# Moving two small transpose steps, and the copies and scan that go with them, from the middle of a projection group to a group boundary

## The reference

```python
u = rmsnorm_2(h, norm_a_g[i])
proj = u @ w_in_a[i]
q, k, v, f_logit, gate = jnp.split(proj, [...], axis=-1)   # 1024, 1024, 1024, 16, 1024 columns
q = rmsnorm_2(q...); k = rmsnorm_2(k...)                   # per head of 64
log_f = jax.nn.log_sigmoid((f_logit + b_forget[i]).astype(jnp.float32))
...
c = jnp.cumsum(log_f, axis=1)                              # decay sums over 512 tokens, 16 heads
logits = logits + ci[..., :, None] - c_k[..., None, :]     # in fox_attention
```

## Time and profile before

| | |
|---|---|
| median of 3 runs | 1868.83 us (1868.81 to 1870.37) |
| the profiled execution | 1868.83 us, its span 1866.9 us |
| mean granted TensorE clock | 0.951 of full speed |
| PE busy | 1731.6 us, 93% of the span |
| DVE, ACT, POOL busy | 915.0, 711.3, 376.2 us |

### The profile page before, as it was taken

The page is one execution under the profiler, slowest core; times in us unless marked ns, Lnnn a source line. Parts: engine busy times, 40 slices in busy tenths (PEclk is TensorE's granted clock), DMA queues, the critical chain, the costliest instruction groups (busy, mean ns, idle before and its releaser), DMA issues.

```text
span 1866.9 us, 24733 instructions
## 1 busy us (share of the span) xinstructions
PE 1731.6 (93%) x9327; PEld 1348.7 (72%) x9327; DVE 915.0 (49%) x1634; ACT 711.3 (38%) x1587; POOL 376.2 (20%) x498
## 2 busy tenths in 40 slices
PE   6999788998978999999799999999999999798988
PEld 5888557877674555788688888877887767686766
DVE  3783373224544666334443234334655664366661
ACT  3322474122135666422442223223324553334550
POOL 5440143001213566011000000000102340013320
PEclk9999796999987999999899999998999999898979
DMA  6223121333101221423132233223221003120111
GB/s 177 83 93 125 56 68 62 113 105 98 46 12 43 68 59 45 137 91 113 45 108 95 90 96 107 91 90 113 91 92 46 24 24 137 67 91 24 47 46 46
DMA packets 117779, 147.65 MB, mean 79 GB/s; under 512 B 30684, under 2 KB 63732, under 8 KB 117424
## 3 DMA queue, kind: packets, MB, share of 16 engines
q1 hardware_dynamic: 116608, 145.40, 24.3%
q0 software_dynamic: 992, 0.86, 0.4%
q10 hardware_dynamic: 80, 0.02, 0.0%
HBM read 125.24 MB, written 4.24 MB: 69 GB/s over the span
## 4 chain that ended last, share of the span: by engine, by line
PE 81%; DVE 8%; ACT 8%; issue 3%; POOL 1%; DMA 0%; ACTq 0%; DVEq 0%; POOLq 0%
PE ps L1777 58%; PE ps L2211 3%; PE ps L2018 3%; PE ps L2042 2%; PE ps L2168 2%; ACT pb L766 2%; PE ps L2186 2%; PE ps L2131 1%; PE ps L2061 1%; PE ps L2075 1%; DVE qkt L1272 1%; DVE nm L1242 1%; ACT qkt L785 1%; PE ps L2023 1%; ACT pbf L824 1%
## 5 line engine op out<-in xcount | busy, mean ns | idle before, releaser
L1777 PE MATMUL ps<-spl,ht 128*128 128x512 f32 x2496 | 577.8, 394 | 12.4 <-DVE xk L1502 8.5
L1777 PEld LDWEIGHTS ps<-spl,ht 128*128 128x128 f32 x2496 | 474.0, 190 | 113.2 <-DVE xk L1502 9.0
L1051 DVE TENSOR_TENSOR spl<-raw,spl 128x1024 fp32r<-128x1024 f32 x180 | 234.7, 1346 | 514.6 <-ACT spl L644 514.6
L644 ACT ACTIVATE spl<-raw 128x1024 fp32r<-128x1024 f32 x180 | 180.4, 1051 | 594.9 <-PE ps L1777 594.7
L1777 PE MATMUL ps<-ht,spl 128*128 128x512 f32 x1152 | 263.9, 391 | 2.0 <-DVE spl L1051 2.0
L1777 PEld LDWEIGHTS ps<-ht,spl 128*128 128x128 f32 x1152 | 217.6, 189 | 48.2 <-issue 2.9
L1777 PE MATMUL ps<-spl,uu 128*128 128x512 f32 x768 | 174.4, 389 | 0.0
L1777 PEld LDWEIGHTS ps<-spl,uu 128*128 128x128 f32 x768 | 144.2, 188 | 29.9
L1674 POOL TENSOR_TENSOR sq<-qkv 128x2048 f32<-128x2048 f32 (+1 forms) x15 | 51.5, 3436 | 360.9 <-ACT qkv L678 346.3
L766 ACT ACTIVATE pb<-ps,nm 128x512 f32<-128x512 f32 (+1 forms) x192 | 99.6, 528 | 45.6 <-DVE nm L1242 45.6
L1710 POOL TENSOR_TENSOR pb<-pb,rg 128x512 f32<-128x512 f32 (+3 forms) x160 | 112.7, 721 | 7.5
(11 more groups left out here) (293 smaller groups left out, 2082.9 us busy)
## 6 DMA issues: line engine op xcount, KB each, us to landing
raw<-w_in SPq DMA_DIRECT2D x30, 1024.0 KB, 5.2
raw<-w_mlp_up SPq DMA_DIRECT2D x16, 1024.0 KB, 5.2
raw<-w_mlp_down SPq DMA_DIRECT2D x16, 1024.0 KB, 5.0
raw<-w_in_a SPq DMA_DIRECT2D x16, 1024.0 KB, 5.3
stq<-qkv SPq DMA_DIRECT2D x32, 256.0 KB, 2.7
raw<-w_in_b SPq DMA_DIRECT2D x8, 1024.0 KB, 5.4
raw<-w_proj_diff SPq DMA_DIRECT2D x4, 1024.0 KB, 5.1
stq<-qkv SPq DMA_DIRECT2D x32, 128.0 KB, 2.5
```

The source lines that it names most:

```text
L644: act.activation(SPL[:, n % 2, HI, 2 * k:2 * k + 2], RAW[:, n % 2, 2 * k:2 * k + 2], ACT.Copy).then_inc(hi_done, 4)
L1051: dve.tensor_tensor(SPL[:, n % 2, LO, 2 * k:2 * k + 2], RAW[:, n % 2, 2 * k:2 * k + 2], SPL[:, n % 2, HI, 2 * k:2 * k + 2].bitcast(F32), A ...
L1777: last = pe.matmul(PS[:, b0 + b], left[:, x], right[:, y], start=(kt == 0 and i == 0), stop=(kt == UK * g["units"] - 1 and i == 2))
```

## The change

The hook `between` is removed from every `run`. What it called is called elsewhere:

- PE: `narrow_across` is called at the start of group 3 instead of after the first unit of group 2. `forget_across` is called at the start of group 5 instead of after the first unit of group 4, and PE's wait for the scan follows directly behind its four transposes.
- ACT: `narrow_out` is called at the start of `forget`, at group 3, instead of after the first split in group 2.
- DVE: `decay_sums` is called at the start of group 5, instead of after the first split (and `norm_two`) in group 4.

```diff
@@ scalar
             def forget():
+                narrow_out(NARROW_2)
                 act.wait_ge(f_link, 2)
                 act.activation(FL[:, 3], FL[:, 2], ACT.Exp, scale=-1.0).then_inc(small_act, 1)
-            run(RUNS["fox_in"], primed=True, follow=True, at={0: lambda: narrow_hi(1, 16), 3: forget},
-                between={2: lambda: narrow_out(NARROW_2)})
+            run(RUNS["fox_in"], primed=True, follow=True, at={0: lambda: narrow_hi(1, 16), 3: forget})
@@ vector
-            run(RUNS["fox_in"], primed=True, follow=True, at={0: lambda: narrow_lo(1, 16), 3: forget},
-                between={4: decay_sums})
+            run(RUNS["fox_in"], primed=True, follow=True, at={0: lambda: narrow_lo(1, 16), 3: forget, 5: decay_sums})
@@ tensor
                     last = pe.transpose(PS[0:16, FORGET_BANK, P * t:P * t + P], FL[:, 7, t], IDF[:])
                 last.then_inc(f_tr, 1)
-
-            run(RUNS["fox_in"], at={5: lambda: pe.wait_ge(f_link, N_FORGET)},
-                between={2: lambda: narrow_across(NARROW_2, 1), 4: forget_across})
+                pe.wait_ge(f_link, N_FORGET)
+
+            run(RUNS["fox_in"], at={3: lambda: narrow_across(NARROW_2, 1), 5: forget_across})
@@ every run, of the three engines
-                        if u == 0 and k in between:
-                            between[k]()
```

More of the change, by code:

```diff
@@ L699, in root, with run @@
                     act.activation(RT[:, 0:NT * heads], SS[:, 0:NT * heads], ACT.Sqrt).then_inc(n_rt, 1)
-            def run(groups, hold=(), primed=False, follow=False, first=None, at={}, between={}, norm=0):
+            def run(groups, hold=(), primed=False, follow=False, first=None, at={}, norm=0):
                 units = [(g, u) for g in groups for u in range(g["units"])]
@@ L1167, in evict, with run @@
                     dve.tensor_tensor(x, PS[:, b0:b0 + 4], x, ALU.add).then_inc(freed["dve"], 1)
-            def run(groups, primed=False, follow=False, first=None, at={}, between={}, norm=0):
+            def run(groups, primed=False, follow=False, first=None, at={}, norm=0):
                 units = [(g, u) for g in groups for u in range(g["units"])]
@@ L1840, in _, with run @@
                      "skv": (x_lo, 3 * KT), "sob0": (y_lo, 3 * KT)}
-            def run(groups, norm=0, at={}, between={}):
+            def run(groups, norm=0, at={}):
                 for n, g in enumerate(groups):
@@ L1853, in run @@
                             unit(g, u, g["unit"] + u)
-                        if u == 0 and n in between:
-                            between[n]()
                 if norm:
```

## The result

The changed kernel takes 1882.0 us (median of 4 runs, 1880.8 to 1883.2) against 1869.6 us (4 runs, 1868.8 to 1873.1): ratio 1.0062, 95% interval 1.0045 to 1.0081, so 8 to 15 us slower. It was forecast slower, 1877.1 us with a range up to 1880.5: the direction held, the size was too small and the time lies above the range. The profiled execution took 1879.7 us, less than any of the four timed ones, with a span of 1877.8 us, 10.9 us more than the span before.

What follows compares the result with a forecast made beforehand. PE was taken as the bound, busy 111.00 of 111.00 us in the stage. 1868.83 + 6.85 for waits + 1.40 for one clock fall = 1877.1 us, range 1874.4 to 1880.5.

Steps and rivals of the forecast that it cites:

- The two waits: PE idles 2.05 us at group 3's start and 4.3 us at group 5's; net cost 2.14 + 4.71 = 6.85 us.
- the first place: Start of group 3: PE waits for ACT's copy, queued behind a 2.01 us split; cost +2.14 us.
- The 11.30 us from a restart to the next split: At both boundaries: PE's restart to ACT's next split takes 11.30 us at full clock; 10.88 if the refill is free.
- The clock at the short wait: Group 3's start: nothing added for a clock fall behind PE's wait of 2.05 us.
- the rival with both falls: PE's clock falls at the waits before groups 3 and 5: 1877.1 + 1.40 = 1878.5 us; chance 0.20.
- The clock at the long wait: Group 5's start: clock falls once, late in PE's 4.3 us wait, adding 1.40 us; the other trace case gave 2.16.
- a table load: ACT at group 3: Exp's 1.28 us load expected behind the copy; ahead of it, +3.42 us instead of +2.14.
- DVE's `forget` and the Exp behind it: After group 2: both come no later behind the split's start than before, so no cost.
- The store and SP's next load: After the scan: parts stored 7.75 us later relative to the split's start, but hidden, since SP's next load waits for a split.
- The five instructions behind the scan: DVE, making the three parts: end 7.45 us behind ACT's split start, 0.2 us to spare, no cost.
- E: At a unit's end: the moment ACT's split starts; it returns after 10.88 us with nothing between.
- The rest of the trace moved as a whole: Outside the new idle times and clock loss: a sign of being right, the remaining trace shifted together.

Runs made afterwards that it cites:

- PE kept busy: Changed kernel plus matmuls of no use on PE, 8 ahead of group 3 and 18 ahead of group 5: 1878.6 us, ratio 1.0039.
- scan ahead: Changed kernel with DVE's scan and its five followers moved ahead of the second split of group 4: 1876.9 us, ratio 1.0024.
- both ahead: Changed kernel with ACT's copy ahead of group 2's second split and DVE's scan ahead of group 4's second split: 1873.7 us, ratio 1.0008.
- copy-ahead kernel: Changed kernel with ACT's copy for the banks of group 1 moved ahead of the second split of group 2: 1878.4 us, ratio 1.0038.
- the first place alone: Kernel before with only the narrow transposes moved to group 3's start and ACT's copy behind both splits of group 2: 1877.3 us, ratio 1.0029.

## Why the prediction was right or wrong

**The two waits.** Right, in place, releaser and size. The prediction has 2.14 + 4.71 = 6.85 us without the clock. With PE kept busy the same places cost 2.01 + 4.64 = 6.65 us, and the first place without a fall of the clock (scan ahead) costs 2.04. PE's restarts came 2.17 us (1322.21 to 1324.38) and 4.62 us (1369.93 to 1374.55) behind the split's start, against 2.28 and 4.73. The 11.30 us from a restart to the next split also held: 11.30 us with both ahead (1372.15 to 1383.45). That the second wait came out at exactly 4.3 us has some luck in it: the restart was 0.11 us early, and the transposes ended 0.09 us earlier than was worked out, since they begin 0.28 us ahead of the split (1354.52 against 1354.80 before), not 0.19.

**The clock at the short wait: the step that failed.** "For the wait of 2.05 us I add nothing: none of the rows has a wait of this size behind dense work." The lack of a row was taken for a cost of nothing, though the rival with both falls stood beside it. The clock fell at 1.93 us of idle time in three of four profiles, and it cost 1.6 us. The rival with falls at both waits (0.20) is what happened in the profiled execution, in both profiles of the changed kernel.

**The clock at the long wait: mis-sized.** The term was 1.40 us, "the case in which the fall came late in the wait". The fall came in the middle of it: the clock was 0.50 from 1372.4, 2.1 us ahead of the restart, and then for 4.5 us of work. That is the pattern of the second of the two waits of 4.25 us, with its price of 2.16 us. "The clock is 1.00 while it waits" was read wrongly for that one; in the kernel before, its second half is already at 0.50:

```profile
491.10:493.20 2.10, 0.00 (x0) 0.00 (x0) 2.10 (x10) 0.00 (x0) 0.00 (x0) 0.50 0.00 0
```

Measured: 6.72 - 4.64 = 2.1 us. The copy-ahead kernel, with the same wait of 4.30 us, has a shorter low stretch (0.50 for 3.4 us instead of 6.8) and pays 6.21 us, 1.6 for the clock. So both rows were possible. The argument for the lower one (a full-size unit directly ahead) decided nothing, as such a unit stands ahead in both kernels.

With 1.6 and 2.1 us the sum is 6.65 + 3.7 = 10.3 us, which is the 10.34 us of the stage. The Trainium skill ("TensorE: Matmul & The Clock Gate", Part 1) advises against idle gaps of PE above a stated length, and 1.93 us is well below it. The trace does not agree that a gap below it is safe, so here the measurement decides.

**The base and the range.** The sum was set on 1868.83 us, nearly the lowest time of the kernel before: 18 more runs have a median of 1870.7 us, and go up to 1877.5. The range's upper end of 1880.5 is this base with 11.7 us, which does hold the 10.3 us, and the profiled execution (1879.7 us) lies inside; it had no room for the scatter of the runs, and 1.28 of the 11.7 us is for a table load that did not come ahead of the copy. Both ends should have had the scatter, not the lower alone. The base of 1870.7 us with 10.3 us makes 1881.0 us, and the medians were 1882.0 and 1882.8; the last 1.0 to 1.8 us stay open. (The chances also have a slip: slower sums to 0.91 by the rivals, not 0.92.)

**What was costed at nothing.** DVE's `forget` and the Exp behind it: right, the Exp stays behind DVE's two steps. The store and SP's next load: right, no engine shows a wait for them. The five instructions behind the scan: right in effect, not as told. They were to end at E + 7.45, 0.2 us ahead of the end of POOL's squaring. The first cast took 4.19 us instead of 0.42 in every profile with the scan behind the split, beside POOL's squaring and memset, so that the five ended at E + 11.1 (1381.0). `norm_one` was late by some 3.4 us, and it was hidden, as the split at 1387.98 still waited 4.26 us for PE.

**The rest of the trace moved as a whole:** right for the two profiles of the changed kernel, not for the others. Behind the stage the shift of the kernel with PE kept busy grows from 7.0 to 8.9 us in one place, where the FOX attention ends and its output projection begins; it grows by 0.7 us more later, and shrinks by 1.4 us near the end. The windows (columns as in rows 2) are that stretch of the kernel before, of the changed kernel and of the filled kernel, each moved by its own shift:

```profile
1536.00:1556.00 20.00, 15.08 (x102) 11.94 (x101) 12.72 (x27) 10.53 (x28) 3.03 (x5) 0.91 0.40 148
```

```profile
1547.00:1567.00 20.00, 15.07 (x101) 11.99 (x101) 12.68 (x27) 10.53 (x28) 2.98 (x5) 0.91 0.40 148
```

```profile
1543.00:1563.00 20.00, 15.07 (x88) 11.46 (x88) 12.75 (x27) 10.52 (x28) 2.98 (x5) 0.74 0.35 130
```

The code is the same, and PE is busy for 15.1 us in each, but the clock is 0.74 instead of 0.91 and 88 matmuls start instead of 101. The kernel with the first place alone has 0.66 in its stretch. Its end is 6.5 us late though its stage costs 3.6. In the six edited kernels later stages add 1.1 to 2.9 us in this way. Whether the edit's shift does it is not shown, as single runs of one kernel scatter more than that (1868 to 1878 us for the kernel before, 1873 to 1880 for the first place alone). That scatter does go with the clock, by the mean granted clock that every run has: in the 43 runs of the kernel before, the four below 1869 us have 0.951, and the three above 1876 us have 0.944. In which stages it was lost isn't seen, as only one run of each kernel has a profile. Why the clock falls at some waits of 1.93 us and not at others also stays open: the kernels have the same code up to the wait, and the moments of earlier changes of the clock differ (it had last risen 50.4 us ahead of the wait in the one that kept it, and 49.1 us ahead in each of the three that lost it).

## What to carry to other kernels

Where an engine runs its program in order, as ACT did here (the copy's bank was ready at 1322.44, and the copy began at 1324.12 behind the split), work that the bottleneck engine needs at a boundary must be queued ahead of the work that the same boundary releases; a copy of 0.2 us behind a split of 2 us stalls PE by the split. Price a new wait of PE twice, for itself and for the clock behind it, and where no row shows a wait of that length, bound the clock's share from both sides instead of setting it to zero: here 0 or 1.6 us behind a wait of 1.9 us, and 1.6 to 2.2 us behind 4.3 us. Where such a wait can't be removed, matmuls of no use in it can keep the clock (6.65 against 10.34 us in the stage, one profile; 3.2 us of the whole by the ratios).

## What the runs showed of the hardware

A wait of only 1.93 us between dense stretches was followed by 3.4 us at half clock (1.2 GHz) in three of four profiles, while waits of 1.30 us and 0.31 us, in two profiles each, were followed by none.

A DVE cast of 16x512 float32 to bfloat16 took 4.19 us beside POOL's 3.60 us squaring and its memset (it ended at 1378.72, 0.27 us behind the memset's end), and 0.42 us elsewhere. With the scan ahead the casts came first and kept their 0.41 us, and POOL's squaring took 6.04 us instead of 3.60:

```profile
1370.54 0.41 DVE L1455 CAST c<-cum 16x512 bf16<-16x512 f32 x1
...
1372.97 6.04 POOL L1672 TENSOR_TENSOR sq<-qkv 128x2048 f32<-128x2048 f32 x1 [18.16 <-ACT qkv L678]
1373.20 2.34 DVE L1049 TENSOR_TENSOR spl<-raw,spl 128x1024 fp32r<-128x1024 f32 x2
```

The Trainium skill ("SBUF — State Buffer", "SBUF: two separate sides") says that certain DVE instructions and GpSimd share a pair of ports that one of them holds for its whole instruction, while the other is blocked. Both rows fit it in size: the cast ends just behind POOL's work, and POOL's squaring ends 3.47 us behind the end of the two subtractions (1375.54), close to its own 3.60 us, as if it had been held until then. The page's order, by which the first to start holds the ports, is not what the starts show: the squaring began at 1372.97, ahead of the subtractions at 1373.20 (and inside the last cast), and in the changed kernel the memset began 2.97 us behind the cast and still took the 0.95 us that it takes in the kernel before.
